# The order and the loads at the head of a gated conv and pooling trunk on eight cores

## The chip, the cores and the metric

The kernel runs on the 8 cores of one Trainium2 chip. Each core works on its own prompt of 2,048 rows and on 4 streams of 32 rows (128 rows), with the same weights. The metric is the device time of the slowest core in microseconds (us). Engines: PE is TensorE (matmuls, transposes), ACT ScalarE, DVE VectorE, POOL GpSimd, SP SyncE, which here only issues DMAs. PEclk is the clock granted to TensorE as a share of 2.4 GHz; it has two levels, 1.00 and 0.50 (1.2 GHz).

## The reference

One layer, `D_MODEL` 1024. What matters here is the norm and the input projection with eight sections of 1024 columns, of which the head of the program works on the first 128 columns of six (`xa`, `ba`, `ca`, `za`, `xb`, `zb`):

```python
h = _rmsnorm(x, g_pre)
proj = h @ w_in                                   # (b, L, 8 * 1024)
xa, ba, ca, za, xb, zb, ga, gb = jnp.split(proj, cuts, axis=-1)
u = ca * xa                                       # branch A: conv of width 3 over time
ya = ((ba * conv) * jax.nn.silu(za)) @ w_a_out
d_g = mean_over_window(xb_g) - xb_g               # branch B: windows 2, 4, 8, 16, then w_grp
yb = (mixed * jax.nn.silu(zb)) @ w_b_out
m = jax.nn.sigmoid(ga) * ya + jax.nn.sigmoid(gb) * yb
x1 = x + _rmsnorm(m @ w_o, g_post)
out = x1 + (p @ w_ple) * jax.nn.sigmoid(x1 @ w_pgate)
```

## The kernel before

Each engine runs its own instruction list in the order in which the program was written; semaphores hold an instruction until what it reads has been written. Work is cut into two super-blocks. The first (number 0) has 1,024 prompt rows in two blocks of 512: `k0` (tiles 0 to 3 of 128 rows) and `k1` (tiles 4 to 7). A phase 1 unit (`phase1_unit`) is one column group `j` of 128 columns for one block: six matmul sections of eight 128x512 matmuls (L601), then the element-wise work of both branches.

At the very start nothing is loaded and the normed, transposed rows `hT` don't exist. So the head is written out by hand, behind L1019. Per tile `phase0_ops` gives six steps, called `ld`, `sq`, `rt`, `dd`, `tr`, `hc`: load by SP (L421), square with row sum on ACT (L426), mean on ACT and root on POOL (L400, L404), scale to bf16 on DVE (L434), eight transposes on PE (L444), copy to `hT` on DVE, for tile 2 on ACT (L454, L450). Tiles 0 to 3 are loaded at once. `after` names for tiles 4 to 7 what the load waits for, so that the transfers come one behind another; tile 7 uses tile 4's buffer and also waits until its square and scale have read it. All x loads are 512 KB.

The weights of a section come through a ring of 12 slots: `load_section` makes POOL issue the next one (L316; 512 KB in HBM, cast to 256 KB). Slots 0 to 5 are XA, CA, BA, ZA, XB, ZB of column group 0, used by both blocks; slots 6 to 11 are those of group 1. `phase1_pieces` (`part`, L571) multiplies a section with a stretch of columns of `hT`: `p0` writes the six banks of `k0`, `p1` those of `k1`, in pieces of 128 to 512 columns as tiles become ready. The banks of `k1` are the same six, so a piece of `p1` waits until `k0`'s result has been read from its bank. `warm` issues small matmuls that only keep TensorE busy.

The element-wise work of unit 0 and block `k0` is written by `phase1_unit` with `pre_banks`, and `between` puts head steps among it. Its steps: ACT copies `xa` (L632); DVE multiplies with `ca` into `U` (L635); conv on ACT and DVE (L641, L643, L646); ACT silu of `za` (L651); two DVE products (L653, L655); ACT copies `xb` to `XB` (L658); ACT silu of `zb` (L661); POOL window sum (L680); DVE difference (L692). An engine can't pass an instruction that waits, so where `between` puts a step decides what waits behind it.

The head ends with the last L571 piece; the first L601 matmul, of column group 1, follows. Nothing behind the head is changed.

Of the kernel before, what the change touches and what calls it, by code (L numbers as in the profile page):

```python
# [17 lines left out]
S_XA, S_BA, S_CA, S_ZA, S_XB, S_ZB, S_GA, S_GB = range(8)  # L18
# [93 lines left out]
def build_program():  # L112
# [32 lines left out]
    with st:  # L145
# [36 lines left out]
        def res(name):  # L182
            if name not in R:
                R[name] = Res(name)
            return R[name]
# [3 lines left out]
        ring_res = [res(f"ring{i}") for i in range(N_RING)]  # L189
# [89 lines left out]
        def keep_warm(n):  # L279
            def f(e, d):  # L280
                ins = None
                for _ in range(n):
                    ins = e.matmul(bank(5)[:, 0:128], lhsT=ident_b[:], rhs=ident_b[:], start=True, stop=True)
                d(ins)
            OP('pe', f, reads=[res("ident_b")], writes=[pres[5]])
# [7 lines left out]
        def wblk(t, b):  # L293
            return t[b * 128:(b + 1) * 128, :].rearrange("p (k c) -> p k c", k=8)
# [3 lines left out]
        for sbi in range(len(SBS)):  # L298
            for ph in (1, 2):
                for j in range(8):  # L300
                    if ph == 1:
                        secs = [(sec, wblk(w_in, sec * 8 + j)) for sec in (S_XA, S_CA, S_BA, S_ZA, S_XB, S_ZB)]
                    else:
                        secs = [(0, wblk(w_in, S_GA * 8 + j)), (1, wblk(w_in, S_GB * 8 + j)), (2, wblk(w_a_out, j)), (3, wblk(w_b_out, j))]
# [253 lines left out]
        def phase1_pieces(k):  # L558
            banks = {}

            def piece(sec, c0, c1):
                if sec not in banks:
                    banks[sec] = (S_XA, S_CA, S_BA, S_ZA, S_XB, S_ZB).index(sec)
                    claim(pres[banks[sec]], 1)
                bi = banks[sec]
                sl, slr = section(0, 1, 0, sec)

                def f(e, d):
                    ins = None
                    for kk in range(8):  # L570
                        ins = e.matmul(bank(bi)[:, c0 - k.rel:c1 - k.rel], lhsT=sl[:, kk, :], rhs=hT[:, kk, c0:c1], start=(kk == 0), stop=(kk == 7))  # L571
                    d(ins)
                rr = [res(f"hT_t{t}_{kk}") for t in range(c0 // 128, c1 // 128) for kk in range(8)]
                assert all(r.epoch == 0 for r in rr)
                OP('pe', f, reads=[slr] + rr, writes=[pres[bi]])
            return piece
# [442 lines left out]
            for _ in range(n):  # L1019
                load_section()  # L1020
        k0, k1 = sb_info[0].blocks
        after = {4: ring_res[0], 5: ring_res[2], 6: ring_res[3], 7: ring_res[4]}
        tiles = [phase0_ops(tl, [after[tl.gi]] if tl.gi in after else []) for tl in sb_info[0].tiles]
        ld, sq, rt, dd, tr, hc = ([t[q] for t in tiles] for q in range(6))
        p0, p1 = phase1_pieces(k0), phase1_pieces(k1)

        def seq(*fns):
            def run():
                for fn in fns:
                    fn()  # L1030
            return run

        def part(p, c0, c1, *secs):
            return lambda: [p(sec, c0, c1) for sec in secs]
        warm = lambda n: (lambda: keep_warm(n))
        secs = (S_XA, S_CA, S_BA, S_ZA, S_XB, S_ZB)
# [1 line left out]
            sq[0], rt[0], lambda: load_section([res("land1")]), load_section, dd[0], warm(20), tr[0],  # L1038
            sq[1], rt[1], load_section, dd[1], hc[0], warm(8), tr[1],
            sq[2], rt[2], dd[2], hc[1], warm(12), tr[2],  # L1040
            sq[3], rt[3], load_section, load_section, hc[2], dd[3], warm(10),
            part(p0, 0, 384, S_XA), tr[3], hc[3], part(p0, 0, 384, S_CA), part(p0, 384, 512, S_XA, S_CA), part(p0, 0, 512, S_BA),
            ld[4], ld[5])()
        phase1_unit(0, sb_info[0], 0, k0, pre_banks=list(range(6)), between={
            'xa': seq(sq[4], rt[4], load_section),
            'u': seq(dd[4], part(p0, 0, 512, S_ZA), tr[4], ld[6], ld[7]),
            'conv': seq(hc[4], part(p1, 512, 640, S_XA, S_CA), part(p0, 0, 512, S_XB)),
            'xb': seq(sq[5], part(p0, 0, 512, S_ZB)),
            'win': seq(rt[5], load_section, load_section, dd[5], tr[5], hc[5], part(p1, 640, 768, S_XA, S_CA),
                       part(p1, 512, 768, S_BA, S_ZA, S_XB))})  # L1050
        seq(sq[6], rt[6], load_section, load_section, dd[6], tr[6], hc[6], part(p1, 512, 768, S_ZB), part(p1, 768, 896, S_XA),
            sq[7], rt[7], load_section, load_section, dd[7], tr[7], hc[7], part(p1, 768, 896, *secs[1:]), part(p1, 896, 1024, *secs))()
        rot['bank:0,1,2,3,4,5,6,7'] = 6
        load_wgrp()
        for sbi in range(nsb):
# [92 lines left out]
```

How the kernel before makes its waits and increments, by code:

```python
            def body(e, ops=ops):  # L99
                for waits, emit, clk, inc in ops:
                    for c, v in waits:
                        e.wait_ge(sems[c], v)
                    if emit is None:
                        continue
                    sem = sems[clk]
                    emit(e, lambda ins, sem=sem, inc=inc: ins.then_inc(sem, inc))
```

## Time and profile before

| | us |
|---|---|
| median of 3 runs | 788.49 (788.14 to 812.35) |
| the profiled execution | 787.21 |
| its span on the slowest core (core 4) | 785.7 |
| span of the eight cores | 779.5 to 785.7 |
| PE busy | 758.3 (97%) |
| DVE, ACT, POOL busy | 339.3 (43%), 259.8 (33%), 323.1 (41%) |

The span runs from the first instruction to the last on one core; the execution's own time lies 1.5 us above it. Busy PE says that matmuls are under way, not that they run at full clock. What is read here is the head of core 4, its first 55.5 us: a row of the timeline has the start, the length from the first to the last end, the engine, line and work, and in brackets how long the engine was idle before it and whose work ended that. Matmul ends are modelled, and consecutive rows overlap. Some matmul records are missing (x87 for 88).

### The profile page before, as it was taken

What the parts mean: (1) busy time and instruction counts of PE and PEld (TensorE: products, weight loads), DVE (VectorE), ACT (ScalarE), POOL (GpSimd) and SP (SyncE); (2) the same over time, 40 slices, a digit from 0 to 9 for tenths busy, and PEclk for the clock granted to TensorE, in tenths of its full rate; (3) what the DMA queues carried; (4) which work ended last, traced back from release to release, by engine and by line L of the source; (5) the groups of instructions that cost most, each with busy time, mean ns of one, the idle gap of its engine ahead of it and who ended that gap; (6) DMA issues with size and microseconds to landing.
All of it is one profiled execution on the core that took longest, in us unless ns stands there. A gap on an engine that the chain in (4) does not pass through costs nothing.

```text
span 785.7 us, 13503 instructions; the slowest of 8 cores (779.5 to 785.7 us)
## 1 busy us (share of the span) xinstructions
PE 758.3 (97%) x4208; PEld 380.2 (48%) x4283; DVE 339.3 (43%) x532; ACT 259.8 (33%) x458; POOL 323.1 (41%) x466
## 2 busy tenths in 40 slices
PE   7589999999999999999999999999999999999996
PEld 5364444444444444444454555545555555554443
DVE  4255544454521122399644545455452222115544
ACT  4322222223233321455432233232331111225554
POOL 3153244546744443254532334545563332213452
PEclk9899999999999999999999999999999999999999
DMA  8588566566797569556243257432454553001432
GB/s 167 171 132 150 82 100 111 91 104 108 131 189 176 116 95 221 109 172 216 95 72 52 42 81 112 68 58 38 82 104 104 79 83 54 2 1 57 158 108 108
DMA packets 36839, 82.41 MB, mean 105 GB/s; under 512 B 4250, under 2 KB 5539, under 8 KB 36772
## 3 DMA queue, kind: packets, MB, share of 16 engines
q0 software_dynamic: 26960, 48.31, 38.8%
q1 hardware_dynamic: 9812, 33.24, 12.9%
q8 instruction: 38, 0.62, 0.3%
q14 instruction: 29, 0.24, 0.1%
HBM read 120.57 MB, written 9.27 MB: 165 GB/s over the span
## 4 chain that ended last, share of the span: by engine, by line
PE 92%; DMA 2%; issue 2%; DVE 1%; ACT 1%; POOL 0%; DVEq 0%; SPq 0%; ACTq 0%; POOLq 0%
PE ps L601 42%; PE ps L765 30%; PE ps L821 7%; PE ps L875 6%; PE ps L571 2%; PE ps L724 2%; DMA arena<-xp 2%; PE ps L886 1%; PE ps L859 1%; DMA ring<-w_in 1%; ACT hb L426 0%; DVE hb L434 0%; DVE hb L898 0%; PE ps L920 0%; DVE hT L511 0%
## 5 line engine op out<-in xcount | busy, mean ns | idle before, releaser
L601 PE MATMUL ps<-hT,ring 128*128 128x512 bf16 (+1 forms) x1800 | 332.6, 345 | 1.3
L601 PEld LDWEIGHTS ps<-hT,ring 128*128 128x128 bf16 x1824 | 162.1, 98 | 168.7
L765 PE MATMUL ps<-hT,ring 128*128 128x512 bf16 (+1 forms) x628 | 122.7, 346 | 0.6
L316 POOL DMA_DIRECT2D ring<-w_in x128 | 69.7, 545 | 93.5 <-PE ps L601 60.3
L787 DVE TENSOR_TENSOR arena<-ps,arena 128x512 f32<-128x512 f32 (+1 forms) x40 | 24.5, 612 | 150.1 <-PE ps L765 109.7
L765 PEld LDWEIGHTS ps<-hT,ring 128*128 128x128 bf16 x640 | 57.6, 98 | 60.3
L680 POOL TENSOR_TENSOR arena<-XB 128x526 f32<-128x526 f32 (+1 forms) x40 | 40.1, 1001 | 113.2 <-ACT XB L658 99.3
L795 POOL TENSOR_TENSOR mT<-arena 128x512 bf16<-128x512 f32 (+1 forms) x40 | 44.2, 1107 | 102.6 <-DVE arena L791 101.6
L902 POOL TENSOR_TENSOR arena<-hb,arena 128x512 f32<-128x512 f32 x30 | 50.8, 1696 | 40.7 <-DVE hb L898 39.4
L777 ACT ACTIVATE arena<-ps 128x512 f32<-128x512 f32 (+1 forms) x40 | 21.3, 533 | 134.1 <-PE ps L765 134.1
L765 PE MATMUL ps<-qT,ring 128*128 128x512 bf16 (+1 forms) x315 | 65.1, 346 | 0.3
L765 PE MATMUL ps<-vT,ring 128*128 128x512 bf16 (+1 forms) x313 | 64.5, 346 | 0.4
L680 POOL TENSOR_TENSOR arena<-arena 128x524 f32<-128x524 f32 (+5 forms) x60 | 59.1, 984 | 9.6 <-POOL arena L680 2.9
L821 PE MATMUL ps<-wo_sb,mT 128*128 128x512 bf16 x265 | 60.8, 379 | 0.4
L641 ACT ACTIVATE arena<-U,vecT 128x512 f32<-128x512 f32 (+1 forms) x40 | 29.9, 749 | 92.6 <-DVE U L635 92.6
L692 DVE SCALAR_TENSOR_TENSOR qT<-arena,XB 128x512 bf16<-128x512 f32 (+1 forms) x40 | 24.6, 616 | 67.8 <-POOL arena L680 61.7
L404 POOL TENSOR_TENSOR stats<-stats,mhalf 128x1 f32<-128x1 f32 x34 | 20.9, 616 | 58.5 <-ACT stats L400 52.9
L765 PEld LDWEIGHTS ps<-vT,ring 128*128 128x128 bf16 x320 | 29.0, 98 | 30.2
L765 PEld LDWEIGHTS ps<-qT,ring 128*128 128x128 bf16 x320 | 29.0, 98 | 30.2
L643 DVE SCALAR_TENSOR_TENSOR arena<-U,vecT,arena 128x512 f32<-128x512 f32 (+1 forms) x40 | 26.9, 672 | 37.2 <-ACT arena L641 37.2
L821 PEld LDWEIGHTS ps<-wo_sb,mT 128*128 128x128 bf16 x272 | 26.0, 98 | 29.0
L736 DVE SCALAR_TENSOR_TENSOR qT<-ps,vecT,mT 128x512 bf16<-128x512 f32 (+1 forms) x40 | 25.0, 666 | 34.8 <-PE ps L724 34.6
(93 smaller groups left out, 743.1 us busy)
## 6 DMA issues: line engine op xcount, KB each, us to landing
ring<-w_in POOLq DMA_DIRECT2D x128, 256.0 KB, 5.0
arena<-xp SPq DMA_DIRECT2D x32, 512.0 KB, 5.2
yp<-arena SPq DMA_DIRECT2D x16, 512.0 KB, 2.9
ring<-w_a_out POOLq DMA_DIRECT2D x16, 256.0 KB, 5.1
ring<-w_b_out POOLq DMA_DIRECT2D x16, 256.0 KB, 5.1
wo_sb<-w_o POOLq DMA_DIRECT2D x8, 256.0 KB, 4.5
wpg_sb<-w_pgate POOLq DMA_DIRECT2D x8, 256.0 KB, 4.7
U<-xT SPq DMA_DIRECT2D x3, 512.0 KB, 5.5
```

The lines of the kernel that those rows point to most:

```text
L316: OP('pool', lambda e, d: d(e.dma_start(out=ring[:, slot, :, :], in_=ring_seq[i])), reads=list(after), writes=[ring_res[slot]], dma=f"ring ...
L601: ins = e.matmul(bank(bi)[:, 0:N], lhsT=sl[:, kk, :], rhs=hT[:, kk, k.rel:k.rel + N], start=(kk == 0), stop=(kk == 7))
L641: OP('act', lambda e, d: d(e.activation(out=cv, in_=uwin(U, k, 16, E), func=AF.Identity, bias=cbias, scale=cw(2))), reads=[ur, sm], writes ...
L643: OP('dve', lambda e, d: d(e.scalar_tensor_tensor(out=cv, in0=uwin(U, k, 15, E - 1), scalar=cw(1), in1=cv, op0=ALU.mult, op1=ALU.add)), re ...
L680: d(e.tensor_tensor(out=twin(out_i, k, nlo, E), in0=a, in1=b_, op=ALU.add))
L692: OP('dve', lambda e, d: d(e.scalar_tensor_tensor(out=actview(qT, j, k), in0=twin(t_sw, k, 16, E), scalar=1.0 / W, in1=uwin(XB, k, 16, E), ...
L736: OP('dve', lambda e, d, bb=bb, jj=jj, k=k: d(e.scalar_tensor_tensor(out=actview(qT, jj, k), in0=blkview(bank(bb), k), scalar=vecT[:, jj, ...
L765: ins = e.matmul(bank(bi)[:, 0:N], lhsT=sl[:, kk, :], rhs=act[:, kk, k.rel:k.rel + N], start=(kk == 0), stop=(kk == 7))
L795: OP('pool', lambda e, d: d(e.tensor_tensor(out=mT[:, j, k.rel:k.rel + N], in0=tap(s.ta)[:, 0:N], in1=tap(s.tb)[:, 0:N], op=ALU.add)), rea ...
L821: ins = e.matmul(ps[s.q][:, h * 512:(h + 1) * 512], lhsT=mT[:, kk, tl.rel:tl.rel + 128], rhs=wo_sb[:, kk, h * 512:(h + 1) * 512], start=(k ...
L875: ins = e.matmul(bank(s.bg[h]), lhsT=x1T[s.xi][:, kk, :], rhs=wpg_sb[:, kk, h * 512:(h + 1) * 512], start=(kk == 0), stop=(kk == 7))
L902: OP('dve' if last else 'pool', lambda e, d: d(e.tensor_tensor(out=wap(s.ow)[:, h * 512:(h + 1) * 512], in0=sig[s.tg[h]], in1=wap(s.ow)[:, ...
```

## The change

The loads of tiles 4 to 7 wait for something earlier: tile 4 for the landing of tile 3 (was ring slot 0), tile 5 for slot 0 (was 2), tile 6 for slot 2 (was 3), tile 7 for slot 3 (was 4) and, as before, for its buffer. The third ring load behind tile 3's root (slot 5) is issued at once instead of after tile 4's root. Norm steps of tiles 4 to 6 move ahead of element-wise steps of unit 0, transposes 4 and 5 stand between the sections BA, ZA and XB, the sections ZA, XB and ZB of `k0` come before any piece of `k1`, and the pieces of `k1` for tiles 4 and 5 are of 256 columns throughout.

```diff
-        after = {4: ring_res[0], 5: ring_res[2], 6: ring_res[3], 7: ring_res[4]}
+        after = {4: res("land3"), 5: ring_res[0], 6: ring_res[2], 7: ring_res[3]}
...
-            sq[3], rt[3], load_section, load_section, hc[2], dd[3], warm(10),
-            part(p0, 0, 384, S_XA), tr[3], hc[3], part(p0, 0, 384, S_CA), part(p0, 384, 512, S_XA, S_CA), part(p0, 0, 512, S_BA),
-            ld[4], ld[5])()
+            ld[4], ld[5], sq[3], rt[3], load_section, load_section, load_section, hc[2], dd[3], warm(10),
+            part(p0, 0, 384, S_XA), tr[3], hc[3], part(p0, 0, 384, S_CA), part(p0, 384, 512, S_XA, S_CA),
+            sq[4], rt[4], dd[4], ld[6], ld[7], part(p0, 0, 512, S_BA))()
         phase1_unit(0, sb_info[0], 0, k0, pre_banks=list(range(6)), between={
-            'xa': seq(sq[4], rt[4], load_section),
-            'u': seq(dd[4], part(p0, 0, 512, S_ZA), tr[4], ld[6], ld[7]),
-            'conv': seq(hc[4], part(p1, 512, 640, S_XA, S_CA), part(p0, 0, 512, S_XB)),
-            'xb': seq(sq[5], part(p0, 0, 512, S_ZB)),
-            'win': seq(rt[5], load_section, load_section, dd[5], tr[5], hc[5], part(p1, 640, 768, S_XA, S_CA),
-                       part(p1, 512, 768, S_BA, S_ZA, S_XB))})
-        seq(sq[6], rt[6], load_section, load_section, dd[6], tr[6], hc[6], part(p1, 512, 768, S_ZB), part(p1, 768, 896, S_XA),
-            sq[7], rt[7], load_section, load_section, dd[7], tr[7], hc[7], part(p1, 768, 896, *secs[1:]), part(p1, 896, 1024, *secs))()
+            'xa': seq(sq[5], rt[5], load_section, load_section),
+            'u': seq(dd[5], tr[4], part(p0, 0, 512, S_ZA), tr[5]),
+            'conv': seq(hc[4], hc[5], part(p0, 0, 512, S_XB, S_ZB)),
+            'win': seq(sq[6], load_section, load_section, rt[6], part(p1, 512, 768, *secs[:5]))})
+        seq(dd[6], tr[6], hc[6], part(p1, 512, 768, S_ZB), part(p1, 768, 896, *secs[:3]),
+            sq[7], rt[7], load_section, load_section, dd[7], tr[7], hc[7], part(p1, 768, 896, *secs[3:]), part(p1, 896, 1024, *secs))()
```

On PE, from the last piece of 128 columns of `k0` on (L571 are section pieces, 128x512 x8 one whole section of `k0`; L444 x8 is one tile's transposes):

```order
 L571 MATMUL ps<-hT,ring 128x384 x8
 L571 MATMUL ps<-hT,ring 128x128 x16
+L571 MATMUL ps<-hT,ring 128x512 x8
+L444 MATMUL ps<-ident_b,hb 128x128 x8
+L571 MATMUL ps<-hT,ring 128x512 x8
+L444 MATMUL ps<-ident_b,hb 128x128 x8
 L571 MATMUL ps<-hT,ring 128x512 x16
-L444 MATMUL ps<-ident_b,hb 128x128 x8
-L571 MATMUL ps<-hT,ring 128x128 x16
-L571 MATMUL ps<-hT,ring 128x512 x16
-L444 MATMUL ps<-ident_b,hb 128x128 x8
```

The transposes of tiles 4 and 5 stand behind BA and behind ZA, with XB and ZB on end behind them; before, tile 5's stood behind ZB, and pieces of `k1` between.

On ACT, from the copy of tile 2 to `hT` on (L426 and L400 are a tile's square and mean, L632 to L661 unit 0's steps):

```order
 L450 COPY hT<-ps 128x8x128
-L632 COPY arena<-ps 128x512
-L426 ACTIVATE hb,stats<-arena 128x1024
-L400 ACTIVATE stats<-stats,epsc 128x1
-L641 ACTIVATE arena<-U,vecT 128x512
-L651 ACTIVATE arena<-ps 128x512
-L658 COPY XB<-ps 128x512
-L426 ACTIVATE hb,stats<-arena 128x1024
-L661 ACTIVATE mT<-ps 128x512
-L400 ACTIVATE stats<-stats,epsc 128x1
```

That is before; the change has in the same place on ACT:

```order
+L426 ACTIVATE hb,stats<-arena 128x1024
+L400 ACTIVATE stats<-stats,epsc 128x1
+L632 COPY arena<-ps 128x512
+L426 ACTIVATE hb,stats<-arena 128x1024
+L400 ACTIVATE stats<-stats,epsc 128x1
+L641 ACTIVATE arena<-U,vecT 128x512
+L651 ACTIVATE arena<-ps 128x512
+L658 COPY XB<-ps 128x512
+L661 ACTIVATE mT<-ps 128x512
```

Tile 4's square stands ahead of the `xa` copy now and tile 5's behind it, ahead of the conv, where it stood behind the copy of `XB`.

On DVE, from tile 3's copy to `hT` on (L434 scales, L454 copies):

```order
 L454 COPY hT<-ps 128x8x128
-L635 TENSOR_TENSOR U<-ps,arena 128x512
 L434 SCALAR_TENSOR_TENSOR hb<-arena,stats,row_bc 128x1024
-L643 SCALAR_TENSOR_TENSOR arena<-U,vecT,arena 128x512
-L646 SCALAR_TENSOR_TENSOR arena<-U,vecT,arena 128x512
-L454 COPY hT<-ps 128x8x128
-L653 TENSOR_TENSOR arena<-ps,arena 128x512
-L655 TENSOR_TENSOR vT<-arena 128x512
+L635 TENSOR_TENSOR U<-ps,arena 128x512
 L434 SCALAR_TENSOR_TENSOR hb<-arena,stats,row_bc 128x1024
```

Scale 4 stands ahead of `U`'s product and scale 5 behind it; the conv's two steps, the copies of tiles 4 and 5 and the products come behind scale 5.

## Rows read from the trace of the kernel before

**Rows 1.** The cores query: span and mean granted clock of two cores.

```profile
core 4: 785.7 us, clock 0.991
core 5: 779.5 us, clock 0.996
```

**Rows 2.** Timeline, PE, core 5: start, length, line, work; the first L601.

```profile
49.04 12.25 PE L601 MATMUL ps<-hT,ring 128*128 128x512 bf16 x56
```

**Rows 3.** Timeline, PE, core 4: start, length, line, work, [idle before, releaser].

```profile
16.20 1.46 PE L571 MATMUL ps<-hT,ring 128*128 128x384 bf16 x8 [0.69 <-ACT hT L450]
...
27.83 0.76 PE L444 MATMUL ps<-ident_b,hb 128*128 128x128 bf16 x8 [4.07 <-DVE hb L434]
...
40.60 0.61 PE L444 MATMUL ps<-ident_b,hb 128*128 128x128 bf16 x8 [3.61 <-DVE hb L434]
42.26 5.08 PE L571 MATMUL ps<-hT,ring 128*128 128x128 bf16 x40 [1.05 <-DVE hT L454]
...
50.36 5.08 PE L571 MATMUL ps<-hT,ring 128*128 128x128 bf16 x88
55.49 4.70 PE L601 MATMUL ps<-hT,ring 128*128 128x512 bf16 x21
```

**Rows 4.** Timeline, PE, core 4, later: 18 sections on end.

```profile
88.08 31.24 PE L601 MATMUL ps<-hT,ring 128*128 128x512 bf16 x142
```

**Rows 5.** Windows, core 4: busy us of engines, granted clock, DMA share, GB/s.

```profile
11.70:15.20 3.50, 3.32 (x39) 3.12 (x37) 3.42 (x5) 1.65 (x5) 2.19 (x4) 1.00 0.93 131
15.20:25.00 9.80, 7.81 (x61) 4.54 (x59) 1.97 (x3) 2.46 (x4) 0.20 (x1) 1.00 1.05 242
28.10:34.90 6.80, 5.22 (x30) 3.03 (x28) 2.89 (x5) 0.00 (x0) 0.00 (x0) 0.50 0.73 233
```

**Rows 6.** Timeline and DMA, SP, core 4: loads of tiles 3, 4, 5; us to landing.

```profile
2.81 0.52 SPq L421 DMA_DIRECT2D arena<-xp  x1
arena<-xp SPq DMA_DIRECT2D x1, 512.0 KB, 8.9
...
15.22 0.33 SPq L421 DMA_DIRECT2D arena<-xp  x1
arena<-xp SPq DMA_DIRECT2D x1, 512.0 KB, 8.6
...
18.83 0.33 SPq L421 DMA_DIRECT2D arena<-xp  x1
arena<-xp SPq DMA_DIRECT2D x1, 512.0 KB, 6.2
```

**Rows 7.** Timeline, ACT, core 4: square of tile 5, then the ZB copy.

```profile
35.89 1.06 ACT L426 ACTIVATE hb<-arena 128x1024 bf16<-128x1024 f32 x1
...
37.09 0.60 ACT L661 ACTIVATE mT<-ps 128x512 bf16<-128x512 f32 x1
```

**Rows 8.** Timeline and DMA, POOL, core 4: ring slots 0 and 3; us to landing.

```profile
8.64 0.75 POOL L316 DMA_DIRECT2D ring<-w_in  x1 [0.35 <-issue]
ring<-w_in POOLq DMA_DIRECT2D x1, 256.0 KB, 6.5
...
14.29 0.57 POOL L316 DMA_DIRECT2D ring<-w_in  x1
ring<-w_in POOLq DMA_DIRECT2D x1, 256.0 KB, 6.1
```

**Rows 9.** DMA, core 5: tile 4's load, issued among ring loads.

```profile
arena<-xp SPq DMA_DIRECT2D x1, 512.0 KB, 5.6
```

**Rows 10.** Timeline, DVE, core 4: unit 0's conv behind tile 4's scale, then the copy.

```profile
27.60 0.74 DVE L643 SCALAR_TENSOR_TENSOR arena<-U,vecT,arena 128x512 f32<-128x512 f32 x1
...
29.11 0.68 DVE L454 COPY hT<-ps 128x1024 bf16<-128x1024 bf16 x1
```

**Rows 11.** Timeline, PE, core 0: tile 4's transpose; windows: the clock after it.

```profile
27.03 0.61 PE L444 MATMUL ps<-ident_b,hb 128*128 128x128 bf16 x8 [2.92 <-DVE hb L434]
...
29.40:32.80 3.40, 3.40 (x21) 2.28 (x22) 0.89 (x2) 0.00 (x0) 0.00 (x0) 0.50 1.00 375
```

## The prediction

> **What bounds the kernel now.** The page's table shows TensorE (PE) busy nearly throughout, so I looked for the places where it waits, and first at what parts the cores. The first L601 matmul marks the end of the head. From it to the end of the span core 4, the slowest, takes 785.7 - 55.5 = 730.2 us, core 5, the fastest, 779.5 - 49.0 = 730.5 [rows 1 to 3]. Both need the same 730 us behind the head, and what parts them is the head, 55.5 against 49.0. The time of this kernel is the head of its slowest core plus a constant, and the change touches the head alone.
>
> Then the PE rows of the head on core 4. Between 16.2 and 55.5 us, 39.3 us pass [rows 3]. The work in them is twelve sections of eight 128x512 matmuls' worth, at 31.24 / 18 = 1.74 us each [rows 4], 20.8 us, and five transposes, each eight instructions of 128 columns, 0.46 us by 5.08 / 11 [rows 3], 2.3 us: 23 us in all. The other 16 us are waits before the transposes of tiles 4 and 5 (4.07 and 3.61 us), shorter ones for the copies behind them (1.05 for tile 5's), and a slow clock after each long wait: 0.50 granted in 28.1 to 34.9 us, the level of 1.2 GHz [rows 5].
>
> What is late first is data. Tile 4 (arena<-xp) is issued at 15.22 us, after ring slot 0 lands, and lands 8.6 us later, at 23.8 [rows 6]. Then come square, mean, root and scale, and its transpose starts at 27.83 [rows 3]: a chain of 4.0 us behind the landing. Tile 5 landed at about 25.0 (18.83 + 6.2) [rows 6], but its square starts only at 35.89 [rows 7], since ScalarE (ACT) has the XB copy ahead of it, and that waits for the XB section, which PE has behind tile 4's pieces. That serial pass, tile 4, then XB, then tile 5, is what is removed.
>
> **The change, part by part.** No matmul work is dropped. Of the second block, XA and CA came in two pieces of 128 columns for tiles 4 and 5 and come in one of 256 now: the same columns. On PE the order is BA, transpose 4, ZA, transpose 5, XB, ZB, then the second block.
>
> *Loads.* Tile 4 now waits for tile 3's landing, about 11.7 us (2.81 + 8.9) [rows 6], not for ring slot 0 (8.64 + 6.5 = 15.1) [rows 8]: 3.5 us earlier. Tile 5 waits for slot 0, so it is issued where tile 4 was. The nearest rows for an x tile among ring loads are 5.6 us on core 5, 6.2 and 8.6 [rows 6, 9]. For tile 4 they give 17.3 to 20.3; I take 18.5, in the lower half, since only 131 GB/s moved in 11.7 to 15.2 us, against 242 from there to 25 [rows 5]. For tile 5 the bounds are 15.1 + 6.2 = 21.3 and 15.1 + 8.6 + 1.7 = 25.4, the 1.7 being one more transfer in front of it (slots 1 to 4 and tiles 4 and 5, six transfers, landed between 15.1 and 25.0, 1.65 us each). I take 15.1 + 8.6 = 23.7, the row of the same instant on the same core: tile 4 is ahead of it now, but moves in the stretch in which little moved.
>
> The Trainium skill (DMA: Bandwidth & Descriptors, Issuing engines are not separate DMA queues) says that transfers issued by different engines run on the same 16 DMA engines and interleave, which speaks against an earlier load being free. By that rule the trace agrees: 8.6 us with more ring loads beside the tile, 6.2 with fewer [rows 6].
>
> *Order.* On ACT the squares of tiles 4 and 5 come ahead of unit 0's conv and its two last copies, so tile 5 no longer waits for XB. On GpSimd (POOL) their roots stand behind the three ring issues at once. On VectorE (DVE) scale 5 stands ahead of L643, so unit 0's conv, both hT copies and its products now wait for tile 5. Behind scale 5 lie the conv, 1.51 us from 27.60 to 29.11, and two copies of 0.68 [rows 10], 2.9 us, while PE runs transpose 5, XB and ZB for 4.0 us: both copies are hidden, and without that cover the five pieces would wait 2.9 us. Ring slots 6 and 7 are issued behind root 5, at about 26 us, and 10 and 11 behind root 7, at about 37. With the slowest load here, 8.6, these land by 46, and the first section that needs slot 10 comes four sections, 6.9 us, after the head's end. They cost nothing.
>
> *Sum, core 4.* L = 23.7 is tile 5's landing. Transpose 5 starts at L + 4.0, by the chain above, 27.7. Transpose 0.5, XB and ZB 3.5: ZB ends at L + 8.0 = 31.7. Then the ZB copy, 0.60 us, with tile 6's square behind it at +0.7 [rows 7], and the chain of 4.0 again: transpose 6 at +4.7. The five pieces take 5 x 0.87 = 4.35 of that, so PE waits about 0.3. From transpose 6 to the pieces behind its copy 1.66 us, as from 40.60 to 42.26 [rows 3]; three pieces of 128 columns 1.4; transpose 7 and three more 1.8; the last six 2.75. Together 4.7 + 1.66 + 1.4 + 1.8 + 2.75 = 12.3. With a full clock the head ends at L + 8.0 + 12.3 = L + 20.3 = 44.0 us.
>
> *Clock.* Transpose 4 comes at 18.5 + 4.0 = 22.5. ZA needs slot 3, which landed at 20.4 (14.29 + 6.1) [rows 8] and has one x tile more in front of it now: 22.0. So ZA runs from 23.0 to 24.7, and PE then waits 3.0 us for transpose 5. On core 0 a wait of 2.92 us was followed by 3.4 us at 0.50, on core 4 one of 4.07 by 6.8 us of it [rows 3, 5, 11]. The wait here is nearest to core 0's. A slow stretch costs half its length where PE has work, as it has from transpose 5 on. Bounds 0 and 3.4 us; I take core 0's, 1.7. The head ends at 45.7.
>
> The gain is 55.5 - 45.7 = 9.8 us. The profiled execution took 787.21 us (1.5 above its span), which gives 777.4. The median of the runs, 788.49, lies 1.3 above the profiled one, so I forecast 778.7.
>
> **The rivals.**
>
> *Tile 5 early, no slow clock.* Tile 5 takes 6.2 us, L = 21.3; the wait before its transpose is 25.3 - 24.7 = 0.6 us and the clock holds. The head ends at 41.6, the time is 774.6. For it: 5.6 us on core 5. Against it: the slowest of eight cores counts, and core 4's own row at that instant is 8.6. 15%.
>
> *The transfers collide.* Tiles 4 and 5 pass among slots 0 to 5, L = 25.4, and the slow stretch is the long one: 25.4 + 20.3 + 3.4 = 49.1, 782.1. For it: the DMA share is 0.93 and 1.05 from 11.7 to 25 us [rows 5], so an earlier byte pushes another back. The skill's rule above is this rival's. 17%.
>
> *No change in effect.* The gain comes back as a wait behind the head, such as for slots 6 to 11: 786 to 790. Against it: the last of these slots follow root 7 as before, and the first come earlier. 5%.
>
> *Slower.* Tile 4's early load starves slot 0. XA can't start, and tile 5, which waits for slot 0, is late by as much. With a long slow stretch the break-even is L = 55.5 - 20.3 - 3.4 = 31.8, which is slot 0 at 31.8 - 8.6 = 23.2 instead of 15.1. One x tile in front is 1.65 us, a fifth of that. With slot 0 at 26 us it would be 791. 3%.
>
> **How the numbers follow.** My forecast, a head of 44 to 47.5 us and 777 to 780.5, has 60%. It is the likeliest, hence 778.7. The range 775 to 783.5 holds it, about half of the early case and most of the collision: some 80%. Two per cent, about what a measurement of this kernel can tell from no change, is 15.8 us: 772.7 needs the head at 39.7, an L of 19.4 with a full clock, which is 4.3 us behind slot 0 where no row is below 5.6: 4%. Slower than 804 needs far more than the last rival gives: 2%. Within 2%: 94%.
>
> **What the changed profile would show.** The first L601 near 45.7 us on the slowest core, and span less that start still 730.2 to 730.5. Tile 4 issued near 11.7 and tile 5 near 15; transpose 5 about 4.0 us behind tile 5's landing; no wait over 0.5 us before the five pieces of 256 columns; one short stretch at 0.50 granted at about 28 to 33 us. The prediction is wrong if tile 5 lands after 26, if PE waits over 1 us for a ring slot at XA, XB or ZB, if the clock falls twice, or if the 730 us behind the head change.

## The result and the profile after

The changed kernel takes 779.1 us in the median of five executions (778.4 to 779.9), against 787.9 for the kernel before. An execution in which the cores of one die ran several per cent longer at a lower granted clock, as that of 812.35 us before, is left out of all times and ratios here. The ratio is 0.989, with a 95% interval of 0.9875 to 0.9913: some 9 us less, with the forecast of 778.7 inside the spread. All cores became shorter in the profiled execution, and the slowest is now core 7. Cores query of the changed kernel: span and mean granted TensorE clock.

```profile
core 0: 775.9 us, clock 0.998
...
core 2: 776.4 us, clock 0.999
...
core 4: 775.5 us, clock 0.998
core 5: 771.8 us, clock 0.998
...
core 7: 776.8 us, clock 0.999
```

Core 4 had 785.7 us at 0.991 and core 5 had 779.5 at 0.996 [rows 1]. The clock is nearly whole on every core now. The head of core 7, from the timeline of PE (start, length, line, work, and in brackets the idle time before with its releaser):

```profile
17.77 1.46 PE L571 MATMUL ps<-hT,ring 128*128 128x384 bf16 x8 [0.18 <-ACT hT L450]
...
24.68 0.61 PE L444 MATMUL ps<-ident_b,hb 128*128 128x128 bf16 x8 [1.08 <-DVE hb L434]
25.12 1.89 PE L571 MATMUL ps<-hT,ring 128*128 128x512 bf16 x8
28.14 0.61 PE L444 MATMUL ps<-ident_b,hb 128*128 128x128 bf16 x8 [1.13 <-DVE hb L434]
28.58 7.98 PE L571 MATMUL ps<-hT,ring 128*128 128x512 bf16 x56
36.64 0.61 PE L444 MATMUL ps<-ident_b,hb 128*128 128x128 bf16 x8
...
39.63 0.61 PE L444 MATMUL ps<-ident_b,hb 128*128 128x128 bf16 x8
40.08 3.85 PE L571 MATMUL ps<-hT,ring 128*128 128x128 bf16 x66
46.08 0.51 PE L571 MATMUL ps<-hT,ring 128*128 128x128 bf16 x6 [2.15 <-issue]
46.42 3.83 PE L601 MATMUL ps<-hT,ring 128*128 128x512 bf16 x17
```

Against core 4 before [rows 3], slowest core against slowest core: the waits of 4.07 and 3.61 us before the transposes of tiles 4 and 5 are 1.08 and 1.13, and that of 1.05 for tile 5's copy is gone. From 28.58 on, XB, ZB and the five pieces of 256 columns run as one row of 56 matmuls. The first L601 starts at 46.42 instead of 55.49: 9.07 us, the whole gain. One row is new. Six matmuls before the end of the head PE stands still for 2.15 us, and the releaser is "issue": PE waits for nothing that the profile shows. The PE waits of core 7 from 15 to 50 us (line, releaser: us in total, times, longest) hold, beside two of 0.2 us, only these:

```profile
PE ps L444 <- DVE hb L434: 2.2, 2, 1.1
PE ps L571 <- issue: 2.1, 1, 2.1
```

The two loads on core 7, from the timeline and DMA rows of SP (issue time; then KB and us to landing):

```profile
12.52 0.33 SPq L421 DMA_DIRECT2D arena<-xp  x1
...
arena<-xp SPq DMA_DIRECT2D x1, 512.0 KB, 8.2
...
15.65 0.33 SPq L421 DMA_DIRECT2D arena<-xp  x1
...
arena<-xp SPq DMA_DIRECT2D x1, 512.0 KB, 8.5
```

Tile 4 lands at 20.7 and tile 5 at L = 24.2. From these rows on four cores (us):

| core | tile 4 lands | L, tile 5 lands | transpose 5 | PE's stop | first L601 | L + 20.3 + stop |
|---|---|---|---|---|---|---|
| 0 | 20.67 | 23.81 | 27.78 | 1.60 | 45.51 | 45.7 |
| 2 | 20.87 | 24.58 | 28.55 | 1.33 | 46.23 | 46.2 |
| 4 | 20.14 | 23.60 | 27.96 | 1.05 | 45.37 | 45.0 |
| 7 | 20.69 | 24.17 | 28.14 | 2.15 | 46.42 | 46.6 |

On the four others tile 5 lands by 20.5, its transpose follows ZA, and the head ends at 41.5 to 42.6. Two of these wait for the ring slot of XB, core 1 for 0.64 us and core 6 for longer:

```profile
25.86 7.98 PE L571 MATMUL ps<-hT,ring 128*128 128x512 bf16 x56 [1.33 <-DMA ring<-w_in]
```

Span less first L601 is 730.1 to 730.4 us on all eight cores. Which cores are slow changes from one execution to the next.

### The profile page after: what moved, and what is told of

The parts are those of the page before. It is cut to its first block, busy times and chain, and to the rows that moved or that the text cites. A ratio compares the mean times of both kernels' runs of the same rounds, so it can differ in the third digit from the quotient of the medians.

```text
span 776.8 us, 13546 instructions; the slowest of 8 cores (771.8 to 776.8 us)
## 1 busy us (share of the span) xinstructions
PE 759.0 (98%) x4267; PEld 378.3 (49%) x4267; DVE 340.4 (44%) x532; ACT 260.2 (33%) x458; POOL 323.0 (42%) x466
## 4 chain that ended last, share of the span: by engine, by line
PE 94%; DMA 3%; issue 1%; DVE 1%; ACT 1%; SPq 0%; POOL 0%; DVEq 0%; ACTq 0%; POOLq 0%
PE ps L601 43%; PE ps L765 30%; PE ps L821 8%; PE ps L875 6%; DMA arena<-xp 2%; PE ps L724 2%; PE ps L571 2%; PE ps L886 2%; PE ps L859 1%; DMA ring<-w_in 1%; DVE hb L898 0%; PE ps L920 0%; DVE hT L511 0%; PE ps L444 0%; DVE hb L931 0%
## 5 line engine op out<-in xcount | busy, mean ns | idle before, releaser
L601 PE MATMUL ps<-hT,ring 128*128 128x512 bf16 (+1 forms) x1824 | 335.2, 345 | 0.0
L601 PEld LDWEIGHTS ps<-hT,ring 128*128 128x128 bf16 x1824 | 162.2, 98 | 168.7
L787 DVE TENSOR_TENSOR arena<-ps,arena 128x512 f32<-128x512 f32 (+1 forms) x40 | 24.4, 611 | 149.4 <-PE ps L765 109.4
L795 POOL TENSOR_TENSOR mT<-arena 128x512 bf16<-128x512 f32 (+1 forms) x40 | 44.3, 1109 | 102.9 <-DVE arena L791 102.3
L692 DVE SCALAR_TENSOR_TENSOR qT<-arena,XB 128x512 bf16<-128x512 f32 (+1 forms) x40 | 24.6, 616 | 68.1 <-POOL arena L680 61.9
L404 POOL TENSOR_TENSOR stats<-stats,mhalf 128x1 f32<-128x1 f32 x34 | 20.7, 610 | 57.5 <-ACT stats L400 51.9
L765 PEld LDWEIGHTS ps<-vT,ring 128*128 128x128 bf16 x320 | 28.9, 98 | 30.2
L765 PEld LDWEIGHTS ps<-qT,ring 128*128 128x128 bf16 x320 | 28.9, 98 | 30.2
L791 DVE TENSOR_TENSOR arena<-ps,arena 128x512 f32<-128x512 f32 (+1 forms) x40 | 24.4, 611 | 36.2 <-PE ps L765 35.2
```

The source lines that it names most:

```text
L601: ins = e.matmul(bank(bi)[:, 0:N], lhsT=sl[:, kk, :], rhs=hT[:, kk, k.rel:k.rel + N], start=(kk == 0), stop=(kk == 7))
L692: OP('dve', lambda e, d: d(e.scalar_tensor_tensor(out=actview(qT, j, k), in0=twin(t_sw, k, 16, E), scalar=1.0 / W, in1=uwin(XB, k, 16, E), ...
L765: ins = e.matmul(bank(bi)[:, 0:N], lhsT=sl[:, kk, :], rhs=act[:, kk, k.rel:k.rel + N], start=(kk == 0), stop=(kk == 7))
L795: OP('pool', lambda e, d: d(e.tensor_tensor(out=mT[:, j, k.rel:k.rel + N], in0=tap(s.ta)[:, 0:N], in1=tap(s.tb)[:, 0:N], op=ALU.add)), rea ...
```

## Experiments

**The loads alone.** The kernel before, with the new table of what each load waits for and nothing else.

```diff
-        after = {4: ring_res[0], 5: ring_res[2], 6: ring_res[3], 7: ring_res[4]}
+        after = {4: res("land3"), 5: ring_res[0], 6: ring_res[2], 7: ring_res[3]}
```

> The kernel before with the changed waits of the loads of tiles 4 to 7 alone; the order of all engines is the old one. My theory (the serial pass, tile 4, XB, tile 5, is the larger part, and the loads only move its start): tile 4 lands at 20 to 21 us as in the changed kernel, and the head ends 30 to 32 us behind that as on every core of before (core 5: 18.9 to 49.0), so at 51 to 53 us on the slowest core and a time 2.5 to 4.5 us below before, ratio 0.994 to 0.997. Rival (the earlier loads carry the gain): head near 46 us, ratio 0.989.

Measured: 784.4 us, ratio 0.996 (0.9946 to 0.9973), as the theory had it. PE on its slowest core, 5:

```profile
26.11 0.61 PE L444 MATMUL ps<-ident_b,hb 128*128 128x128 bf16 x8 [0.29 <-DVE hb L434]
28.44 6.17 PE L571 MATMUL ps<-hT,ring 128*128 128x128 bf16 x32 [1.73 <-DVE hT L454]
38.23 0.61 PE L444 MATMUL ps<-ident_b,hb 128*128 128x128 bf16 x8 [3.62 <-DVE hb L434]
```

Tile 4 landed at 20.50 and tile 5 at 24.13, as early as in the changed kernel. Yet transpose 5 starts at 38.23, 14 us behind the landing, after the same 3.6 us of waiting as before: its square still stands behind the XB copy. Only what tile 4 gained arrives. It landed at 17.9 to 20.5 over the cores, against 18.9 to 23.8 before. The head of core 5 ends at 54.26, not at 51 to 53: the profiled execution, with 786.2 us, was the longest of the six.

**The order alone.** The changed kernel with the old table: the line above the other way round.

> The changed kernel with the old waits of the loads of tiles 4 to 7; the order is the new one. My theory: tile 4 lands at 23.8 us, transpose 4 comes at 27.8, ZA ends at 30.0, transpose 5 then finds tile 5 ready, ZB ends at 34, and the head ends 12.3 us later plus a stop of 1 to 2 us near its end (see e3) and 0 to 3.4 us of slow clock after the wait of 4 us: 47.5 to 51 us, ratio 0.991 to 0.995. Rival (the order is worth nothing without the loads): head at 54 us or later, ratio 0.998 to 1.002.

Measured: 783.7 us, ratio 0.9953 (0.9937 to 0.9969), at the upper end of what was expected. PE on its slowest core, 2:

```profile
24.23 0.61 PE L444 MATMUL ps<-ident_b,hb 128*128 128x128 bf16 x8 [1.67 <-DVE hb L434]
...
31.35 1.01 PE L444 MATMUL ps<-ident_b,hb 128*128 128x128 bf16 x8 [4.79 <-DVE hb L434]
32.16 9.73 PE L571 MATMUL ps<-hT,ring 128*128 128x512 bf16 x56
...
51.39 0.51 PE L571 MATMUL ps<-hT,ring 128*128 128x128 bf16 x6 [2.15 <-issue]
51.95 4.44 PE L601 MATMUL ps<-hT,ring 128*128 128x512 bf16 x12
```

Here it is tile 5 that PE waits for, which the expectation had as ready: it landed at 27.38, against 24.98 on core 4 before, transpose 5 came 3.97 us later, and the 56 matmuls took 9.73 us instead of 7.98, since the clock was at 0.5 from 28.9 to 35.7 us. L + 20.3 + 1.75 + 0.4 (the slow transpose) + 2.15 = 52.0, measured 51.95. On cores 0 and 7 it was as expected: one wait of 4.7 and 5.2 us before transpose 4 and none before transpose 5. So the order brings the chain that hangs on L alone, and the loads bring an early L. By the ratios the loads alone give 3.1 us, the order alone 3.7 and both together 8.3. Whether the 1.5 us beyond the plain sum are real the intervals, 1.1 to 1.5 us to either side of each figure, do not settle.

**Fewer loads in flight when PE stops.** In after, a 16 KB packet on the DMA queue that the profile calls "instruction" starts 2.3 to 2.6 us before PE goes on, on all eight cores. On core 7 it starts at 43.67, and PE goes on at 46.08; on core 0 at 42.85 and 45.17. DMA query of after, core 0, 42.8 to 43.9 us (queue: packets, MB, share of 16 engines):

```profile
q0 software_dynamic: 281, 0.14, 111.5%
q8 instruction: 1, 0.02, 5.4%
```

One packet, amid the ring loads. The experiment moves the issues of ring slots 8 to 11, and of the weights `w_grp` behind them, behind later steps.

```diff
-            'win': seq(sq[6], load_section, load_section, rt[6], part(p1, 512, 768, *secs[:5]))})
+            'win': seq(sq[6], rt[6], part(p1, 512, 768, *secs[:5]))})
...
-            sq[7], rt[7], load_section, load_section, dd[7], tr[7], hc[7], part(p1, 768, 896, *secs[3:]), part(p1, 896, 1024, *secs))()
+            sq[7], rt[7], load_section, load_section, dd[7], tr[7], hc[7], lambda: load_section(hres_tile(sb_info[0].tiles[7])), load_section, part(p1, 768, 896, *secs[3:]), part(p1, 896, 1024, *secs))()
```

> The changed kernel with ring slots 8 and 9 issued behind root 7, 4 us later, and slots 10 and 11 and w_grp behind tile 7's copy to hT, 4 us later. It asks what the stop of PE of 0.8 to 2.1 us is, that the changed kernel has on all eight cores before its 321st matmul, a few pieces ahead of the head's end, with no semaphore behind it and a 16 KB transfer on the instruction queue that starts 2.3 us before PE goes on. Theory A (the fetch of PE's next instructions stands in the DMA engines behind the ring loads): with fewer of these in flight from 33 to 41 us it comes earlier, the stop is under 0.5 us on all cores, the head ends at 44.5 us on the slowest core, and the time is 1 to 2 us below the changed kernel's. Theory B (the fetch is asked for late and takes its own time): the stop stays at 0.8 to 2.1 us, and the time is the changed kernel's.

Measured: 776.1 us, ratio 0.986 (0.9842 to 0.9878): 3 us below the changed kernel (2.7 by the ratios), where 1 to 2 were expected. The stop is gone on all eight cores. PE and the same DMA query (41.1 to 42.2 us), core 0:

```profile
39.53 0.61 PE L444 MATMUL ps<-ident_b,hb 128*128 128x128 bf16 x8
39.98 4.18 PE L571 MATMUL ps<-hT,ring 128*128 128x128 bf16 x72
44.00 3.18 PE L601 MATMUL ps<-hT,ring 128*128 128x512 bf16 x14
```

```profile
q0 software_dynamic: 40, 0.05, 27.3%
q8 instruction: 1, 0.02, 5.4%
```

The 66 and 6 matmuls are one row of 72. On this core the packet starts at 41.19 instead of 42.85, though the last transpose is later than in after (39.53 against 39.27), and the ring moves 40 packets around it, not 281. It comes 2.5 us ahead of the matmul at which PE stopped: just in time. Counted in PE's records, the packet starts when PE has begun 274 to 282 matmuls, on every core; in after it starts at 296 to 319. So loads in flight delay this packet, and PE stands until it has come. The length of the packet goes the same way: on core 0 of the kernel with the order alone it took 1.9 us instead of 0.9 to 1.2, and PE went on 3.2 us after its start. All this rests on pairing in time and on this experiment; no row shows when the packet was asked for, or for which engine.

**Sixteen matmuls fewer ahead of it.** The idle matmuls that keep PE busy (L283) are cut from 22 to 6 behind transposes 1 and 2.

```diff
-            sq[2], rt[2], dd[2], hc[1], warm(12), tr[2],
-            ld[4], ld[5], sq[3], rt[3], load_section, load_section, load_section, hc[2], dd[3], warm(10),
+            sq[2], rt[2], dd[2], hc[1], warm(6), tr[2],
+            ld[4], ld[5], sq[3], rt[3], load_section, load_section, load_section, hc[2], dd[3],
```

> The changed kernel with 16 of the 50 matmuls that only keep TensorE busy left out (6 of 12 behind transpose 1, all 10 behind transpose 2): PE's list is 16 matmuls shorter ahead of the head's end. If the stop belongs to a place in PE's list of instructions (theory of the fetch), it stands before the 321st matmul again, which is now the 11th of L601, and as ten matmuls of 216 ns stand ahead of it where 57 ns ones did, it is shorter by 1.6 us: 0 to 0.5 us, and the head ends 1 to 2 us earlier. If it belongs to the work there (a bank, a copy), it stays before the same piece and as long. If the clock needs these matmuls, XA runs at 0.50 and the head is later by 0.7 us or more.

Measured: 778.3 us, ratio 0.9887 (0.9871 to 0.9902), no different from the changed kernel. PE, core 0, first XA's piece and then the end of the head:

```profile
16.21 2.72 PE L571 MATMUL ps<-hT,ring 128*128 128x384 bf16 x8 [1.25 <-ACT hT L450]
...
44.02 2.10 PE L601 MATMUL ps<-hT,ring 128*128 128x512 bf16 x9
47.22 2.98 PE L601 MATMUL ps<-hT,ring 128*128 128x512 bf16 x13 [1.10 <-issue]
```

In after the stop stands 6 matmuls before L601. With 16 fewer ahead it stands 9 into L601, before the 320th matmul: the place hangs on PE's list of instructions, to within one matmul, and not on the work. Five cores stopped for 0.27 to 1.10 us, the others not at all, where at most 0.5 was expected. The head did end earlier, by 44.3 us on the last core instead of 46.4, but the stop now comes behind it. The third branch of the expectation came too: XA's eight matmuls took 2.72 us, as at half the clock, where they take 1.46 in after (the record of the granted clock begins only behind them, at 20.9 us). That cost core 0 nothing, as PE waits 1.84 us for transpose 4 in after and not at all here.

**Sixteen more.** warm(10) became warm(26). The time is that of a single execution.

> The changed kernel with 16 warming matmuls more behind transpose 2 (26 for 10). The other side of e4_fewer_warm: if the stop belongs to a place in PE's list, it stands before the 321st matmul again, which is 16 matmuls earlier in the program (between pieces of tile 7's columns), and is as long or longer, 1 to 3 us; if it belongs to the work, it stays before the same piece. The warming matmuls themselves end before or up to 0.5 us behind the copy that XA waits for.

Measured: 778.8 us. Core 3, the slowest with 777.3, and core 0:

```profile
40.27 3.01 PE L571 MATMUL ps<-hT,ring 128*128 128x128 bf16 x51
45.68 0.51 PE L571 MATMUL ps<-hT,ring 128*128 128x128 bf16 x6 [2.40 <-issue]
```

```profile
41.08 4.18 PE L571 MATMUL ps<-hT,ring 128*128 128x128 bf16 x72
45.10 1.24 PE L601 MATMUL ps<-hT,ring 128*128 128x512 bf16 x5
```

Where PE stops, it does so 21 matmuls before L601, 15 earlier in the work than in after, before the 322nd of the list. But only core 3 stops, with the packet at 43.20. On the other seven it starts at 32.4 to 39.8, long before the need. Only PE's list differs from the changed kernel's, so this moved the packet, which speaks for its being PE's. That all cores would stop for 1 to 3 us was a miss, and it tells something of the change. The groups of PE by form, core 0, 0 to 60 us, of before and then of after (the idle before and its releaser at the end):

```profile
L571 PE MATMUL ps<-hT,ring 128*128 128x128 bf16 x144 | 10.4, 238 | 3.0 <-DVE hT L454 2.8 <-PE ps L571 0.2
...
L571 PE MATMUL ps<-hT,ring 128*128 128x256 bf16 x32 | 5.8, 357 | 0.0
```

```profile
L571 PE MATMUL ps<-hT,ring 128*128 128x128 bf16 x112 | 6.9, 219 | 1.8 <-issue 1.6 <-PE ps L571 0.2
...
L571 PE MATMUL ps<-hT,ring 128*128 128x256 bf16 x48 | 5.6, 273 | 0.0
```

The change makes 32 matmuls of 128 columns into 16 of 256: the same columns, but 16 matmuls fewer, each with its weight load. In the kernel before, the 321st matmul stood 22 ahead of L601, and in the changed kernel 6 ahead. Sixteen more idle matmuls put the place back to 21 or 22, and the stop goes from seven cores, as it was on none in the kernel before and in the one with the loads alone, which have it at 22 as well. So two things bring it: the place in the list, which the merged pieces moved, and the loads in flight. Why the packet then starts so much earlier, and why core 3 still stops, is open.

**Tile 4 earlier still.**

```diff
-        after = {4: res("land3"), 5: ring_res[0], 6: ring_res[2], 7: ring_res[3]}
+        after = {4: res("land1"), 5: ring_res[0], 6: ring_res[2], 7: ring_res[3]}
```

> The changed kernel with tile 4's load waiting for tile 1's landing (8 us) instead of tile 3's (12 us). My theory (from 12 us on the DMA engines are full, so an earlier load pushes another back): tile 4 lands about 1 to 2 us earlier and ring slots 0 to 2 later by up to 1.7 us, and with slot 0 tile 5's issue; the head is within 1.5 us of the changed kernel's and the ratio to before 0.988 to 0.992. Rival (the wait for tile 4 is what counts): transpose 4 earlier by 2 us, the head too, ratio 0.986 to 0.987.

Measured: 782.6 us, ratio 0.9941 (0.9922 to 0.9959): some 4 us worse than the changed kernel, which neither theory had. PE on core 5, whose head ends last, and its clock (window, PE busy, the other engines, granted clock, DMA share, GB/s):

```profile
23.48 0.61 PE L444 MATMUL ps<-ident_b,hb 128*128 128x128 bf16 x8
23.93 1.89 PE L571 MATMUL ps<-hT,ring 128*128 128x512 bf16 x8
30.27 0.61 PE L444 MATMUL ps<-ident_b,hb 128*128 128x128 bf16 x8 [4.45 <-DVE hb L434]
30.71 9.67 PE L571 MATMUL ps<-hT,ring 128*128 128x512 bf16 x56
```

```profile
30.80:34.30 3.50, 3.50 (x11) 1.23 (x9) 3.24 (x5) 0.00 (x0) 0.00 (x0) 0.51 0.98 123
```

Tile 4 was issued at 9.42, ahead of ring slot 0 at 9.95, and landed at 14.8. Slot 0 landed at 16.7, so tile 5 was issued at 16.76 and, with the ring loads beside it, took 9.5 us: L = 26.30. Transpose 4 then needed no wait, ZA was done early, and the whole delay stood as one wait of 4.45 us before transpose 5. The clock fell to 0.51, which cost the 56 matmuls 9.67 - 7.98 = 1.7 us. L + 20.3 + 1.7 + 1.3 (the stop) = 49.6, measured 49.42. Tile 5's landing sets the head; tile 4's only decides whether the waiting is split in two.

**Both loads earlier, with the late ring.** The kernel with slots 8 to 11 moved, and one line more.

```diff
-        after = {4: res("land3"), 5: ring_res[0], 6: ring_res[2], 7: ring_res[3]}
+        after = {4: res("land2"), 5: res("land3"), 6: ring_res[2], 7: ring_res[3]}
```

> The kernel of e3_late_ring with tile 4's load waiting for tile 2's landing and tile 5's for tile 3's (instead of tile 3's and ring slot 0's). Theory (the head ends 20.3 us behind tile 5's landing, as long as the ring slots for XB and ZB are there): tile 5 is issued 3.5 us earlier and lands at 21 instead of 24 on the slow cores, slots 0 to 5 come 1 to 1.7 us later, transpose 5 is then bound by ZA behind slot 3, ZB by slot 5 at 27 to 28.5: the head ends at 41 to 43 us, 1 to 3 us before e3, and the ratio to before is 0.982 to 0.985. Rival (the DMA engines are the bound already): the slots lose what the tiles gain and the time is that of e3 or above it, 0.986 to 0.989.

Measured: 775.8 us, ratio 0.9854 (0.9838 to 0.987), between the two ranges expected and not told apart from 776.1 without that line. Tile 5's DMA row and PE, core 4:

```profile
arena<-xp SPq DMA_DIRECT2D x1, 512.0 KB, 11.5
```

```profile
22.17 1.67 PE L571 MATMUL ps<-hT,ring 128*128 128x512 bf16 x7 [1.01 <-DMA ring<-w_in]
...
26.77 0.61 PE L444 MATMUL ps<-ident_b,hb 128*128 128x128 bf16 x8 [0.76 <-DVE hb L434]
```

Tile 5 was issued at 11.32, against 15.22 on this core in after, but took 11.5 us and landed at 22.8, against 23.6: of 3.9 us, 0.8 arrive. The latest landing of any core tells the same, 23.3 against 24.1 with the late ring alone. Part of it is paid by a ring slot, which took 11.2 us and for which BA waits 1.0 us now. The stop is back on three cores, for 0.23, 0.23 and 0.78 us, so moving the ring loads took it away only just. As the rule that the prediction weighed has it (the Trainium skill, DMA: Bandwidth & Descriptors, Issuing engines are not separate DMA queues), the loads share 16 engines whoever issues them, and the trace agrees. The two kernels with the late ring are the fastest that ran.

## The prediction, point by point

*The head plus a constant: right.* 730.1 to 730.4 us behind the first L601 on all cores, 730.2 to 730.5 forecast. The first L601 fell by 9.07 us, the median by 8.8.

*Tile 5's landing: right.* 23.7 was forecast, and 23.6 to 24.6 came on the four slow cores; core 4 itself gave 23.60. Issued at 15.1 to 15.7, it took 8.4 to 9.3 us.

*Tile 4's landing: wrong, without harm.* The step argued that tile 4 would take the lower half of the row bounds because only 131 GB/s moved in 11.7 to 15.2 us [rows 5]. It was issued at 11.8 to 12.5 and took 8.2 to 8.8 us on the four slow cores, not 6.8: it landed at 20.1 to 20.9, behind the upper bound of 20.3 on three of the four slow cores. A low GB/s was not free room: the DMA share was 0.93 in that window [rows 5].

*The chain L + 4.0 and L + 20.3: right.* Transpose 5 follows tile 5's landing by 3.97 us on cores 0, 2 and 7, and L + 20.3 with the stop added gives the four heads within 0.4 us. The two hT copies on VectorE stayed under cover: no wait stands before the five pieces. No slow core waits for a ring slot. Two fast cores do, at XB, 0.64 us on core 1 and 1.33 on core 6. A wait of over 1 us there was among the prediction's signs of being wrong, so on core 6 one of them came: with an early tile 5 the weights of XB set the head, which L + 20.3 does not have. It did not reach the time, as that head ends at 42.6.

*The late ring slots: right in the end, with a wrong price.* The slowest load was taken as 8.6 us. Slots 6 and 7 took 10.4 and 12.2 us on core 7, and the weights `w_grp` 12.6. They still cost no wait of their own, as slot 11 landed at 45.8, before 46 as forecast. What they did cost is the next point but one.

*The clock: the term that failed.* One wait of 3.0 us before transpose 5 and a slow stretch costing 1.7 us were forecast. Since tile 4 landed about 2 us later than forecast, ZA ended later, and the delay came as two waits (1.84 and 0.79 us on core 0, 1.08 and 1.13 on core 7). Slot 3, which ZA needs, was late as well: 22.5 to 24.5 on the slow cores, not 22.0, so that on core 7 ZA could not have ended at 24.7 even with an early tile 4. Only core 4 had a slow stretch, before transpose 5, where it cost 0.4 us (27.96 instead of 23.60 + 3.97). Windows of core 4 in after:

```profile
20.80:24.20 3.40, 1.36 (x8) 0.50 (x7) 1.51 (x2) 1.85 (x5) 0.56 (x1) 1.00 1.00 245
24.20:27.60 3.40, 3.40 (x15) 1.75 (x15) 1.83 (x3) 1.69 (x4) 1.62 (x3) 0.50 1.04 257
```

The price of 1.7 us was sound: with tile 4 early, so that there was one long wait, it was 1.7 us on core 5. What was wrong is that the wait would be whole.

*What no step held: PE's stop of 0.8 to 2.15 us before the 321st matmul.* In this execution it is on all eight cores, and took the place of the clock term in the sum: 1.7 forecast, 2.15 found on the slowest core, whose head ends at 46.42, not 45.7. So the number came out as close as it did by luck, by two errors of like size. With the stop gone the kernel takes 776.1 us, and the forecast without its clock term would be 777.0. In the kernel before a 16 KB packet of the same queue started at 50.28 us on core 4, 3.8 us ahead of the 321st matmul (2.8 to 4.9 over the cores), and PE did not stop. The prediction counted the merged pieces as the same columns and priced them at nothing; that they are 16 matmuls fewer in PE's list, it left out. The rival "no change in effect" named a wait for slots 6 to 11 behind the head; what came is a smaller cost of the same loads, ahead of its end.

*The other rivals.* Tile 5 early was true of the four fast cores (landed by 20.5, heads of 41.5 to 42.6), and the slowest core counts, as the prediction had it. Collision in full did not come: L stayed under 25.4 on every core. The slower rival's mechanism is real: with tile 4 issued ahead of slot 0, slot 0 landed at 16.7 and L was 26.3, but this was far from its break-even of 31.8.

## What to carry to other kernels

Where a serial pass holds a chain, an earlier load and a new order pay only in part each; before changing, ask which of the two ends last. An earlier transfer among others in flight arrives earlier by a fraction of the shift, here 0.8 of 3.9 us, and can push back the transfer that the next step waits for; the row to price it by is one from the same instant, not the GB/s of the window. And a stop of an engine with no releaser can be, as here by all that the experiments show, its own instructions arriving late: look for a packet on the instruction queue just ahead, move bulk loads away from it, and mind that a changed count of instructions moves its place.

## What the runs showed of the hardware

- PE stood still up to 2.15 us (2.4 with more idle matmuls) when a 16 KB packet of the "instruction" queue came late among ring loads. That it carries PE's instructions is inferred, from the pairing in time and from its moving with PE's list. The Trainium skill (Runtime: NRT & Kernel Launch, Instruction fetch mechanics) says that instructions are fetched in blocks of 16 KiB on a DMA queue of their own while the engine executes, and that this is mostly hidden. The trace agrees on the packets, 16 KB and 0.92 to 1.22 us each where PE stopped in after, and, in the kernel before, on their being hidden; in after this one was not.
- A long wait does not always bring the slow clock. In the kernel with the order alone, core 4 waited 3.19 us before transpose 5 and no slow stretch followed, while after core 4 of the changed kernel had waited 2.04 us before transpose 4, the clock fell. With the order alone, core 2 had a second slow stretch, of 3.4 us, just behind its stop of 2.15 us; core 7 of the changed kernel had none behind a stop of the same length.
- A 256 KB weight load, 6.1 to 6.5 us in [rows 8], took 10 to 12 us where x tiles and other ring loads were in flight (slots 6 and 7 of core 7).
